# A hybrid decoder layer on one core: the down weights of expert blocks 15 to 26 are issued from ScalarE's DMA queue instead of SyncE's

## The reference

```python
z = rmsnorm(x) @ w_in                       # GDN and sliding-window projections
h = x + concat(gated_deltanet(z), dilated_attention(z)) @ w_out
hn = rmsnorm(h)
logits = hn @ w_router + b_router           # 32 experts, top 4, softmax gates
for each block of tokens of one expert e:   # 32 experts, D_FF = 1024
    gu = xblk @ w_gate_up[e] + b_gate_up[e] # 1024 x 2048
    gate = minimum(gu[:, :1024], 7.0); up = clip(gu[:, 1024:], -7.0, 7.0)
    act = (up + 1.0) * gate * sigmoid(1.702 * gate)
    y = act @ w_down[e] + b_down[e]         # 1024 x 1024
out = h + sum over the 4 experts of a token of gate * y
```

## Time and profile before

| | before |
|---|---|
| median of 3 runs | 1085.18 us (1084.86 to 1085.53) |
| the profiled execution's own time | 1084.44 us |
| its span in the profile | 1082.9 us |
| mean granted TensorE clock | 0.988 |
| TensorE matmul busy | 1020.7 us (94%) |
| VectorE, ScalarE, GpSimd busy | 303.9, 164.2, 21.3 us |
| moved by DMA | 427.64 MB, nearly all on SyncE's queue (q1) |

### The profile page before, as it was taken

How to read it: one execution, slowest core, us unless ns; L and a number is a source line. 1 busy time by engine, 2 the same in 40 slices (tenths; PEclk the granted TensorE clock), 3 DMA queues, 4 the chain that set the end, 5 groups by cost and what they waited for, 6 DMA issues and landing times.

```text
span 1082.9 us, 12842 instructions
## 1 busy us (share of the span) xinstructions
PE 1020.7 (94%) x5096; PEld 449.9 (42%) x5096; DVE 303.9 (28%) x703; ACT 164.2 (15%) x283; POOL 21.3 (2%) x37
## 2 busy tenths in 40 slices
PE   9999999999999999999999889988999888989997
PEld 7888866433434343434343233323333222223232
DVE  4987754312222222222322111111221011111111
ACT  3513436011111110111001010000110001110101
POOL 3201000000000000000000000000000000000000
PEclk9999999999999999999999999999999999999999
DMA  9724779999999999999999999999999999999996
GB/s 328 280 83 161 286 283 368 396 428 429 428 429 432 432 434 432 432 427 428 432 433 427 427 429 430 432 431 428 432 429 433 432 429 430 432 431 435 424 424 283
DMA packets 39036, 427.64 MB, mean 395 GB/s; under 512 B 8251, under 2 KB 10524, under 8 KB 20188
## 3 DMA queue, kind: packets, MB, share of 16 engines
q1 hardware_dynamic: 37840, 426.84, 93.8%
q10 hardware_dynamic: 1164, 0.34, 0.1%
HBM read 424.42 MB, written 2.75 MB: 394 GB/s over the span
## 4 chain that ended last, share of the span: by engine, by line
DMA 50%; PE 44%; DVE 2%; ACT 1%; issue 1%; SPq 0%; ACTq 0%; DVEq 0%
DMA store<-in_w_gate_up_dram 26%; DMA store<-in_w_down_dram 23%; PE bank L2312 14%; PE bank L2375 11%; PE bank L1789 5%; PE bank L1781 3%; PE bank L1916 2%; PE bank L2077 2%; PE bank L2218 2%; PE bank L2227 1%; PE bank L2275 1%; DMA brt<-in_b_router_dram 1%; PE bank L1924 1%; PE bank L2335 1%; DMA store<-in_w_in_dram 1%
## 5 line engine op out<-in xcount | busy, mean ns | idle before, releaser
L2312 PE MATMUL bank<-store,flow 128*64 128x512 f32 x2048 | 451.8, 597 | 19.8 <-DMA store<-in_w_gate_up_dram 19.2
L2312 PEld LDWEIGHTS bank<-store,flow 128*64 128x64 f32 x2048 | 149.6, 138 | 314.2 <-issue 285.9
L2375 PE MATMUL bank<-store,flow 128*64 128x512 f32 x992 | 230.4, 614 | 31.8 <-DMA store<-in_w_down_dram 31.2
L1620 DVE TENSOR_SCALAR flow<-bank 128x512 f32<-128x512 f32 x32 | 22.1, 691 | 605.3 <-PE bank L2312 605.3
L2375 PEld LDWEIGHTS bank<-store,flow 128*64 128x64 f32 x992 | 72.8, 140 | 180.8 <-issue 150.6
L1010 ACT ACTIVATE flow<-flow 128x512 f32<-128x512 f32 x32 | 20.2, 630 | 427.7 <-DVE flow L1620 427.7
L2227 PE MATMUL bank<-qkT 64*128 64x512 f32 x248 | 61.9, 616 | 0.0
L1026 ACT COPY qkT<-bank 128x512 f32<-128x512 f32 x31 | 18.1, 585 | 228.3 <-PE bank L2375 228.3
L1020 ACT COPY flow<-flow 128x512 f32 x30 | 33.7, 1123 | 49.5 <-DVE flow L1596 27.8
L2227 PEld LDWEIGHTS bank<-qkT 64*128 64x128 f32 x248 | 21.3, 186 | 40.1 <-issue 40.1
L1781 PE MATMUL bank<-store 128*128 128x256 f32 x160 | 35.5, 381 | 0.0
(11 more groups left out here) (360 smaller groups left out, 660.0 us busy)
## 6 DMA issues: line engine op xcount, KB each, us to landing
store<-in_w_gate_up_dram SPq DMA_DIRECT2D x50, 4096.0 KB, 28.1
store<-in_w_down_dram SPq DMA_DIRECT2D x57, 2048.0 KB, 21.6
store<-in_w_gate_up_dram SPq DMA_DIRECT2D x26, 2048.0 KB, 13.9
store<-in_w_in_dram SPq DMA_DIRECT2D x6, 2048.0 KB, 13.7
store<-in_w_down_dram SPq DMA_DIRECT2D x9, 1024.0 KB, 25.1
store<-in_w_out_dram SPq DMA_DIRECT2D x1, 4096.0 KB, 14.2
store<-in_w_gate_up_dram SPq DMA_DIRECT2D x3, 1024.0 KB, 7.2
flow<-in_w_down_dram SPq DMA_DIRECT2D x1, 2048.0 KB, 12.1
```

The source lines that it names most:

```text
L1620: dve.tensor_scalar(gt, bank[4][:], LIMIT, None, ALU.min).then_inc(g_min, 1)
L2312: ins = mm(dst[SLOTS * hf:SLOTS * (hf + 1), :], rows[:, c:c + SLOTS], store[:, slot_at(j, odd) + c0:slot_at(j, odd) + c0 + 512], start=fir ...
L2375: ins = mm(dst[SLOTS * hf:SLOTS * (hf + 1), :], turned[:, c:c + SLOTS], w[:, hf * 512:(hf + 1) * 512], start=f == 0, stop=f == KT - 1)
```

## The change

SyncE's loops over blocks 15 to 26 issue only gate-up weights (a new `load_gate_up`, with the waits that `load_block` had). ScalarE's loop over blocks 14 to 25 issues the down weights of the next block, half by half, between `window` and `output`, on its own queue. The waits for `wdn_used` are on the same counts as before. Blocks up to 14 and from 27 on are loaded as before.

```diff
+ACT_LOADS, ACT_LOADS_END = 15, 27
...
+            def load_gate_up(m):
+
+                odd = sp.value_load(parity[0:1, bass.ds(m + 1, 1)], min_val=0, max_val=1)
+                for half in range(2):
+                    sp.wait_ge(wgu_used, 4 * m + (2 * half - 2))
+                    sp.wait_ge(ld_tile[2 * half], 16 * m + 32)
+                    sp.dma_start(half_dst(half, odd), expert_half(bass.ds(m + 1, 1), half)).then_inc(ld_tile[2 * half], 16)
...
-            with sp.Fori(FINE_BLOCKS, LATE_BLOCKS) as b:
+            with sp.Fori(FINE_BLOCKS, ACT_LOADS) as b:
                 load_block(b, b, b + 1, 2, True)
-            with sp.Fori(LATE_BLOCKS, LAST_ORDER) as b:
-                load_block(b, b, b + 1, 1, True)
-            with sp.Fori(LAST_ORDER, N_EXP - 5) as b:
-                load_block(b, b, b + 1, 0, True)
+            with sp.Fori(ACT_LOADS, ACT_LOADS_END) as b:
+                load_gate_up(b)
...
-            with act.Fori(LAST_CHUNKS + 1, two_less) as b:
+
+            with act.Fori(ACT_LOADS - 1, ACT_LOADS_END - 1) as b:
+                gated(b)
+                evacuate(b)
+                window(b + 1)
+                for hf in range(2):
+                    act.wait_ge(wdn_used, 2 * b + (hf + 1))
+                    act.wait_ge(ld_tile[4 + hf], 16 * b)
+                    act.dma_start(tile_dst(4 + hf), expert_tile(bass.ds(b + 1, 1), 4 + hf)).then_inc(ld_tile[4 + hf], 16)
+                output(b, bank[7])
+            with act.Fori(ACT_LOADS_END - 1, two_less) as b:
                 expert_block(b)
```

## The result

The changed kernel takes 1094.55 us (median of 6 runs, 1092.83 to 1098.34) against 1085.31 us before on the same chip: 1.0091 times the time, with a 95% interval of 1.0078 to 1.0104. It is slower by 9.2 us, where I had forecast no change and a range that ended at 1088.8.

The account below looks back on a forecast made before the run. The DMA engines were taken as the bound, TensorE having 4.4 us to spare in each 29.2 us block. Terms 0 + 0 + 0 + 0 on the 1085.18 us median gave 1085.2 us, range 1082.6 to 1088.8.

Parts of the forecast that it names:

- The bound: In the stretches with the changed blocks, DMA engines are full (share 1.00, 429 to 431 GB/s); TensorE has room.
- The issues on ScalarE at 0: 24 down-weight issues added to ScalarE, about 0.38 us each, delay its output copy some 0.5 us, which nothing awaits: cost 0.
- The moved loads: Blocks' down weights arrive early beside gate-up weights on two equal queues; stalls move to gate-up weights, total bytes same: worth 0.
- The price of the hold: Removing the hold of SyncE's down-weight issues on gate-up loads behind them: worth 0, as each half awaits the one before.
- The hand-over at 0 with 2.3 us left over: At block 27 SyncE waits for block 26's `wdn_used`, but issues 2.3 us before the DMA engines run dry: cost 0.
- time T: Landing of block 26's second gate-up half; SyncE may issue at T + 14.5, engines run dry at T + 18.2.
- Rival 1: Faster: two queues move data at a higher rate than one; 1082.8 us, or 1081.6 over all twelve blocks; chance 0.14.
- rival 2: Slower: interleaving two queues costs rate, 2.3 us per cent over 234 us; 1089.9 us at 2%; chance 0.16.
- the 6%: Trainium skill's SBUF page: two concurrent transfers 6% faster than one; over 234 us it would take off 14 us.
- Rival 4: Equal shares do not come about, down weights still trickle in last, stalls stay on them; time 1085.2 us; chance 0.08.
- rival 3: Engines run dry at the block 27 hand-over (1 to 2 us, 1086.7) or in the loop through late ScalarE issues; chance 0.05.

Follow-up runs that it names:

- the paced run: Changed kernel, but SyncE issues the second gate-up half of block m+1 only once block m's first down half has landed (blocks 15 to 26): 1086.39 us, 1.0011.

## Why the prediction was wrong

**The bound was read rightly.** The DMA engines were full before and are full in every stretch of the changed loop, at 428 to 430 GB/s. TensorE's lower clock (0.92 and 0.94 granted against 0.96 and 0.99) and its longer stalls left no mark on the DMA share there, and the paced run, with stalls of up to 7.7 us, is nearly as fast as before.

**The issues on ScalarE at 0: right.** ScalarE's issues take their 0.36 us, and the first of each pair follows TensorE closely (597.53 in the changed kernel, with `down` begun at 593.62). The only wait of TensorE on ScalarE in this stretch is one of 0.2 us, and it was there before; none is on the output copy.

**The moved loads: here it failed.** The step reads "At equal shares both queues have work while 4.19 MB of down weights and as much of gate-up weights move". I took equal shares from no row. The rate of the two queues was the unknown that I bounded; the division of the rate was not bounded at all. The shares were 2 to 1 in bytes (16.15 to 8.36 MB), since they are 1 to 1 in packets (557 to 558) and the packets are 32 and 16 KB. The DMA view of a stretch of before gave the first length (39 packets, 1.28 MB). With the stalls on down weights growing instead of shrinking, the statement that they would move to gate-up weights was wrong too.

**The price of the hold: it failed here too.** I valued at 0 the hold that down-weight issues put on the gate-up loads behind them, reasoning that a gate-up half waits for its predecessor anyway. That wait limits how many are in flight, not how far ahead they are. The old queue's order was what rationed the engines between the two kinds of weights. The paced run, which puts such a hold back, takes back 8 of the 9 us.

**The hand-over at 0 with 2.3 us left over.** The place was right and the price wrong: 8.1 us dry. The sum there rested on TensorE waiting for the second gate-up half of block 26 at time T, with 19.5 us of transfers behind it. In fact both halves of block 27 had landed when the engines fell dry at 944, 11 us before TensorE began on them (954.99), and nothing stood behind.

**The rivals.** Rival 1 and rival 2 (rate) did not come about, nor the 6% that the prediction put with rival 1: 430 GB/s against 431, and 428 against 428 with the same rows on one queue and on two. Rival 4 had the right condition, "equal shares do not come about and down weights still trickle in last", and I gave it 0.08 at a time of 1085.2; rival 3 had the right place and 0.05. Neither was followed to what the other makes of it.

**A label.** What the earlier trace rows and the prediction call block 25 (`gate_up` at 852.73, `down` at 870.46) is block 24: block 26 runs `down` at 929.99, and the blocks before it at 899.10 and 870.46. No term of the sum hangs on the number.

**Open.** The dry 8.1 us leave 1.5 us of the profiled 9.6. Of these, 0.8 lie ahead of ScalarE's first load at 597.53: `down` of block 14 starts at 593.62 against 592.79. About 0.7 us stay unexplained. The spread of the changed kernel's runs (1092.8 to 1098.3, against 1084.2 to 1085.5) stays open; a deficit that depends on how close 143 GB/s is to 143.6 may well vary from run to run, but no run here shows it.

## What to carry to other kernels

On a queue that keeps the DMA engines full, the order of issues is a schedule: whoever takes a part of the loads to a second queue gives that schedule up, and gets (in these runs) one that goes by packet length. Before such a move, read the packets and MB of each kind of load, divide the rate by them, and compare the smaller part with what that load needs in a round; where it doesn't suffice, hold the other queue back with one wait. Engines busy to 1.00 inside a stretch do not mean that the stretch is harmless: look at where both streams meet again.

## What the hardware showed that I had not expected

Two queues on the same engines moved equal numbers of packets while both had work, whatever their lengths: 427 and 421 in 36 us, 557 and 558 in 57 us, 257 and 256 in 18 us, 224 and 222 in 12 us. So the part of the down weights went from 20% over 34 and 51 to 67% with the row lengths alone (gate-up and down rows of 32 and 8, 32 and 16, 16 and 16, 8 and 16 KB).

More DMAs in a full stream cost time although they carry no more data: 24 additional ones, with rows of 16 KB instead of 32 and all on SyncE's queue, 3.3 us, or 0.14 us each; 72 additional ones with 8 KB rows, beside ScalarE's loads, 7.6 us, or 0.11 us each. The page of each counts 16 more packets under 512 B per additional DMA (8635 and 9404 against 8251). The prices are upper bounds: in the two traces the last `down` starts 2.9 and 6.2 us later than before (1072.32 and 1075.61 against 1069.43), which is 0.12 and 0.09 us each, and the rest comes behind it. TensorE's loop is written out in parts in both kernels, and what that costs was not told apart either. Whether the number or the length of the rows costs was not told apart.
